# The tail of a one-core hybrid layer: last down products by column halves, gate rows and final gain spread by TensorE

## The reference, cut to what matters

```python
xf = x + gate1 * mix                                   # x1
h = rmsnorm(xf, norm2_g) * (1 + scale2) + shift2
act = silu(g) * u * combine.T[:, :, None]
routed = einsum('etf,efd->td', act, w_expert_down)
xf = xf + gate2 * (routed + shared)
y = rmsnorm(xf, final_norm_g)
```

## Time and profile before

| what | value |
|---|---|
| median of three runs | 862.09 us (861.97 to 862.58) |
| the profiled execution | 862.36 us, span 860.5 us |
| granted TensorE clock, mean | 0.982 |
| PE busy | 809.0 us (94%) |
| DVE busy | 385.1 us (45%) |
| ACT busy | 238.9 us (28%) |
| DMA read and written | 280.67 MB, 3.16 MB |

### The profile page before, as it was taken

How to read it: one execution, slowest core, us unless ns; L and a number is a source line. 1 busy time by engine, 2 the same in 40 slices (tenths; PEclk the granted TensorE clock), 3 DMA queues, 4 the chain that set the end, 5 groups by cost and what they waited for, 6 DMA issues and landing times.

```text
span 860.5 us, 13102 instructions
## 1 busy us (share of the span) xinstructions
PE 809.0 (94%) x5330; PEld 556.9 (65%) x5330; DVE 385.1 (45%) x789; ACT 238.9 (28%) x397; POOL 20.0 (2%) x22
## 2 busy tenths in 40 slices
PE   3999999999999989999999999699999999799974
PEld 1788989999999979964545445254554835355212
DVE  1157899879987657573232312122221111112014
ACT  2253747535345144231111111011121101011002
POOL 1000010100000010100000000000000000000000
PEclk9999999999999999999999999899999999899998
DMA  8998877432443739978999999999999999999995
GB/s 322 387 387 299 299 271 283 162 125 98 145 150 101 230 119 375 369 294 341 364 415 418 416 417 418 414 418 419 415 417 410 418 413 419 417 417 418 417 414 205
DMA packets 81223, 284.71 MB, mean 331 GB/s; under 512 B 5257, under 2 KB 12041, under 8 KB 64521
## 3 DMA queue, kind: packets, MB, share of 16 engines
q1 hardware_dynamic: 80664, 282.55, 84.5%
q10 hardware_dynamic: 496, 1.30, 0.4%
HBM read 280.67 MB, written 3.16 MB: 330 GB/s over the span
## 4 chain that ended last, share of the span: by engine, by line
PE 72%; SPq 14%; DMA 9%; DVE 3%; issue 2%; ACT 0%; POOL 0%; DVEq 0%; POOLq 0%
PE bank L2118 13%; SPq L620 13%; PE bank L2174 7%; PE bank L1708 6%; PE bank L1713 6%; PE bank L1710 6%; DMA chunk<-in_w_expert_down 5%; PE bank L2002 4%; PE bank L2025 3%; PE bank L1694 3%; PE bank L1770 3%; DMA chunk<-in_w_expert_gate_up 3%; PE bank L1655 3%; PE bank L1752 3%; PE bank L1730 2%; PE bank L1734 2%
## 5 line engine op out<-in xcount | busy, mean ns | idle before, releaser
L2118 PE MATMUL bank<-chunk,xg 128*64 128x512 f32 (+2 forms) x1024 | 202.5, 624 | 19.8 <-DMA chunk<-in_w_expert_gate_up 19.6
L2118 PEld LDWEIGHTS bank<-chunk,xg 128*64 128x64 f32 (+2 forms) x1024 | 62.7, 131 | 153.1 <-issue 137.1
L2174 PE MATMUL bank<-chunk,act_t 128*64 128x512 f32 (+2 forms) x480 | 95.7, 597 | 1.5 <-DMA chunk<-in_w_expert_down 1.5
L1509 DVE SCALAR_TENSOR_TENSOR act_r<-bank,w_slot,sil 128x256 f32<-128x256 f32 x26 | 12.6, 484 | 182.6 <-ACT sil L984 182.6
L984 ACT ACTIVATE sil<-bank 128x256 f32<-128x256 f32 x26 | 10.0, 384 | 211.3 <-PE bank L2118 211.3
L1521 DVE TENSOR_TENSOR y_lo<-bank,y_hi 128x512 fp32r<-128x512 f32 x52 | 35.9, 691 | 72.2 <-ACT y_hi L997 72.2
L1077 DVE TENSOR_TENSOR ring_lo<-ring,ring_hi 128x1024 fp32r<-128x1024 f32 x44 | 52.6, 1219 | 18.3 <-ACT ring_hi L766 18.1
L2174 PEld LDWEIGHTS bank<-chunk,act_t 128*64 128x64 f32 (+2 forms) x480 | 29.6, 127 | 46.9 <-issue 46.0
L997 ACT ACTIVATE y_hi<-bank 128x512 fp32r<-128x512 f32 x52 | 30.9, 597 | 100.5 <-PE bank L2174 95.7
L1137 DVE SCALAR_TENSOR_TENSOR conv<-upad,dw,conv 128x256 f32<-128x256 f32 x120 | 52.8, 511 | 0.0
L766 ACT ACTIVATE ring_hi<-ring 128x1024 fp32r<-128x1024 f32 x44 | 44.4, 1051 | 24.8 <-PE bank L1734 14.9
(11 more groups left out here) (319 smaller groups left out, 1239.2 us busy)
## 6 DMA issues: line engine op xcount, KB each, us to landing
chunk<-in_w_expert_gate_up SPq DMA_DIRECT2D x128, 1024.0 KB, 20.9
chunk<-in_w_expert_down SPq DMA_DIRECT2D x63, 1024.0 KB, 22.7
ring<-in_w_in SPq DMA_DIRECT2D x16, 2048.0 KB, 9.9
ring<-in_w_ada SPq DMA_DIRECT2D x12, 2048.0 KB, 14.8
ring<-in_w_proj_hgrn SPq DMA_DIRECT2D x2, 2048.0 KB, 7.9
ring<-in_w_out SPq DMA_DIRECT2D x2, 2048.0 KB, 13.0
ring<-in_w_proj_conv SPq DMA_DIRECT2D x1, 2048.0 KB, 7.7
chunk<-in_w_shared_gate_up SPq DMA_DIRECT2D x2, 1024.0 KB, 23.0
```

The lines of the kernel that those rows point to most:

```text
L2118: ins = mm(bank[2 + b][row:row + width, :], xg[:, k, c:c + width], w[:, k % 4, :], start=(k == 0), stop=(k == KD - 1))
L2174: ins = mm(out[row:row + width, :], act_t[:, c, row:row + width], w[:, c, h * 512:(h + 1) * 512], start=(c == 0), stop=(c == 1))
```

## The change

1. The last chunk is loaded in two column halves, each holding both contraction halves (128 x 2 pieces of 2 KB). `last_down` makes output half 0 first and reports it, then half 1, with the wait for the second piece in front of the last expert's product of half 1.
2. `finish` on PE scatters half 0, waits for `x1_back`, makes two of the four groups of `x1` transposes, then waits for half 1, scatters it and makes the other two groups. `gated_y` waits for its own half alone.
3. `gate2` and the final gain are no longer loaded in spread form. PE makes the six rows of 512 columns in `final_rows`, between the two gate and up halves of the last step: 24 float32 products of a broadcast column with the identity, in banks 0 and 1 by turns. ACT copies each out.
4. `final_norm_g` becomes a twelfth small load (8 rows), in the place of the convolution's weights. These become the last load on ACT's queue.
5. The DRAM copy of the modulation holds `shift2` alone: one transpose fewer, and half the copy and the store.
6. The `x1` load waits for place 16 alone and is the only load behind the last chunk.

```diff
-R_ALL = 116
+R_FG = 116
+R_ALL = 124
 ...
-                       (by_row(A["conv_norm_b"][0]), rows[R_CNB:R_CNB + 4, :]),
+                       (by_row(A["conv_norm_b"][0]), rows[R_CNB:R_CNB + 4, :]), (by_row(A["final_norm_g"]), rows[R_FG:R_FG + 8, :]),
                        (A["conv_dw_w"][0].rearrange("w (c p) -> (w c) p", p=P), rows_dw[0:CW * CC, :])]
 ...
-                        for c, loaded_half in enumerate((s_chunk[place_of(number)], s_last_half)):
-                            src = dn_src[bass.ds(experts[item], 1)][:, :, c:c + 1, :].rearrange("a p c d -> (a p) c d")
-                            sp.dma_start(dn_tile(place_of(number))[:, c:c + 1, :], src).then_inc(loaded_half, 16)
-            for number in (max(n for n in CHUNK_AT if place_of(n) == at_) for at_ in FINAL_PLACES):
-                freed(number)
-            for s in range(NS):
-                sp.dma_start(g2row[:, s, :].rearrange("p (k c) -> p k c", k=KD), mod_row(1, s)).then_inc(s_g2_back, 16)
+                        for hf, loaded_half in enumerate((s_chunk[place_of(number)], s_last_half)):
+                            c = slice(hf * 512, (hf + 1) * 512)
+                            src = dn_src[bass.ds(experts[item], 1)][:, :, :, c].rearrange("a p c d -> (a p) c d")
+                            sp.dma_start(dn_tile(place_of(number))[:, :, c], src).then_inc(loaded_half, 16)
+            freed(max(n for n in CHUNK_AT if place_of(n) == FINAL_X1))
             sp.dma_start(x1_back[:, :, :].rearrange("p k t -> p (k t)"), A["x1"]).then_inc(s_x1_back, 16)
-            sp.dma_start(fin_g[:, :], A["final_norm_g"].rearrange("(a d) -> a d", a=1).broadcast_to([P, D])).then_inc(s_x, 16)
 ...
                 if n == NSTEPS - 1:
+                    for j in range(6):
+                        c = slice(j % 2 * 512, (j % 2 + 1) * 512)
+                        act.wait_ge(row_made, j + 1)
+                        nc.scalar.activation(g2row[:, j // 2, c] if j < 4 else fin_g[:, c], bank[j % 2][:, :], ACT.Copy).then_inc(row_kept, 1)
 ...
-                    dve.wait_ge(y_done, 3 + s)
+                    dve.wait_ge(y_done, 2 * hf + s + 1)
 ...
-                dve.wait_ge(s_x, 48)
 ...
-                dve.wait_ge(s_g2_back, 32)
+                dve.wait_ge(row_kept, 6)
 ...
+            def final_rows():
+                pe.wait_ge(pt_evac, NSTEPS)
+                for j in range(6):
+                    if j >= 2:
+                        pe.wait_ge(row_kept, j - 1)
+                    s, hf = divmod(j, 2)
+                    for i in range(4):
+                        k = 4 * hf + i
+                        col = mod_v[:, M_GT2 + k, s:s + 1] if j < 4 else vec[:, R_FG + k:R_FG + k + 1]
+                        ins = mm(bank[hf][:, i * P:(i + 1) * P], col.broadcast_to([P, P]), ident, start=True, stop=True)
+                    ins.then_inc(row_made, 1)
 ...
+                    if (n, half) == (NSTEPS - 1, 0):
+                        final_rows()
 ...
-                for h in range(2):
-                    for c in range(2):
-                        for item in range(items - c):
-                            one(h, c, item)
-                pe.wait_ge(s_last_half, 16)
-                for h in range(2):
-                    one(h, 1, items - 1).then_inc(dn_done, 1)
+                for c in range(2):
+                    for item in range(items):
+                        ins = one(0, c, item)
+                ins.then_inc(dn_done, 1)
+                for c in range(2):
+                    for item in range(items):
+                        if (c, item) == (0, items - 1):
+                            pe.wait_ge(s_last_half, 16)
+                        ins = one(1, c, item)
+                ins.then_inc(dn_done, 1)
 ...
-                for h in range(2):
-                    pe.wait_ge(y_ready, 2 * NSTEPS - 1 + h)
-                    for s in range(NS):
-                        scatter(1, s, h, last=True).then_inc(y_done, 1)
+                pe.wait_ge(y_ready, 2 * NSTEPS - 1)
+                for s in range(NS):
+                    scatter(1, s, 0, last=True).then_inc(y_done, 1)
                 pe.wait_ge(s_x1_back, 16)
-                for j in range(4):
+                for j in range(2):
+                    x1_to_tokens(j)
+                pe.wait_ge(y_ready, 2 * NSTEPS)
+                for s in range(NS):
+                    scatter(1, s, 1, last=True).then_inc(y_done, 1)
+                for j in range(2, 4):
                     x1_to_tokens(j)
```

More of the change, by code:

```diff
@@ L82 @@
 FINAL_PLACES = (15, 16, 17)
+FINAL_X1 = 16
 LOADS_BEFORE_EXTRAS = (len(CHUNK_NO) - EXTRA_PLACES) // NCHUNK + 1
@@ L85 @@
 assert len(CHUNK_NO) % NCHUNK >= EXTRA_PLACES
+assert all(max((n, key) for n, key in CHUNK_AT.items() if n % NCHUNK == place)[1][0] == NSTEPS - 2 for place in FINAL_PLACES)
 C_ID, C_MASK = 0, P
@@ L191, in build @@
         c_pad = at("c_pad", 205, [P, KD, 32])
-        mod_cols = at("mod_cols", 205, [NS * KD, 2 * P])
+        mod_cols = at("mod_cols", 205, [NS * KD, P])
         b_router = at("b_router", 207, [P, NE])
@@ L264, in build @@
         mod_v = mod[:, :, :]
-        s_x, s_cst, s_rows, s_s0, s_wr = map(sem, ("x_and_final_gain_loaded", "consts_loaded", "rows_loaded", "s0_then_shift_rows_loaded", "masks_router_and_routing_consts_loaded"))
+        s_x, s_cst, s_rows, s_s0, s_wr = map(sem, ("x_loaded", "consts_loaded", "rows_loaded", "s0_then_shift_rows_loaded", "masks_router_and_routing_consts_loaded"))
         gain1_done, u1_bias_ready, u1_part_ready = map(sem, ("gain1_done", "u1_bias_ready", "u1_bias_rows_made_then_copied"))
@@ L307, in build @@
         s_last_half = sem("last_half_chunk_loaded")
-        g2_ready, g2_evac = sem("gate2_ready"), sem("gate2_evac")
-        s_g2_kept, s_g2_back = sem("gate2_stored"), sem("gate2_loaded")
+        sh2_ready, sh2_evac, s_sh2_kept = sem("shift2_ready"), sem("shift2_evac"), sem("shift2_stored")
+        row_made, row_kept = sem("final_row_made"), sem("final_row_kept")
         cnt_ready, nx_done, end_ready, oh_done = map(sem, ("count_ready", "nx_done", "end_ready", "onehot_done"))
@@ L564, in _ @@
             sp.dma_start(new_state[0, 0].rearrange("a h k v -> k (a h) v"), s_new[:, :, :]).then_inc(s_state, 16)
-            sp.wait_ge(g2_evac, 1)
-            sp.dma_start(A["mod_rows"], mod_cols[:, :]).then_inc(s_g2_kept, 16)
+            sp.wait_ge(sh2_evac, 1)
+            sp.dma_start(A["shift_rows"], mod_cols[:, :]).then_inc(s_sh2_kept, 16)
             def load_fixed(number):
@@ L571, in load_fixed @@
                 load_part(number, part, FIRST_FIXED + sum(ITEMS_OF[:step]) + item)
-            def mod_row(m, s):
-                return A["mod_rows"].rearrange("(k s) (m c) -> s m k c", s=NS, m=2)[s:s + 1, m].broadcast_to([P, KD, P])
             for number in range(NCHUNK):
@@ L579, in _ @@
                     sp.wait_ge(o_ready, 4)
-                    sp.wait_ge(s_g2_kept, 16)
+                    sp.wait_ge(s_sh2_kept, 16)
                     for s in range(NS):
-                        sp.dma_start(shift_row[:, s, :].rearrange("p (k c) -> p k c", k=KD), mod_row(0, s)).then_inc(s_s0, 16)
+                        src = A["shift_rows"].rearrange("(k s) c -> s k c", s=NS)[s:s + 1].broadcast_to([P, KD, P])
+                        sp.dma_start(shift_row[:, s, :].rearrange("p (k c) -> p k c", k=KD), src).then_inc(s_s0, 16)
                 if number == 5:
@@ L884, in _ @@
                             nc.scalar.activation(upad_row[:, c * T:(c + 1) * T], conv[:, c, :], ACT.Sigmoid).then_inc(cs_done, 1)
-            act.wait_ge(g2_ready, 1)
-            nc.scalar.activation(mod_cols[:, :], bank[7][0:NS * KD, 0:2 * P], ACT.Copy).then_inc(g2_evac, 1)
+            act.wait_ge(sh2_ready, 1)
+            nc.scalar.activation(mod_cols[:, :], bank[7][0:NS * KD, 0:P], ACT.Copy).then_inc(sh2_evac, 1)
             act.wait_ge(cb_ready, 1)
@@ L1340, in _ @@
             dve.wait_ge(s_state, 16)
-            dve.wait_ge(s_g2_kept, 16)
+            dve.wait_ge(s_sh2_kept, 16)
             own.mark(V.memset(selm, -BIG))
@@ L1633, in _ @@
             pe.wait_ge(s_cst, 32)
-            pe.wait_ge(s_rows, 16 * 11)
+            pe.wait_ge(s_rows, 16 * 12)
             nc.tensor.transpose(bank[7][:, 0:R_ALL], rows[0:R_ALL, :], ident[0:R_ALL, 0:R_ALL])
@@ L1834, in _ @@
                     pe.wait_ge(mod_done, 7)
-                    nc.tensor.transpose(bank[7][0:NS * KD, 0:P], mod_v[:, M_SH2:M_SH2 + KD, :].rearrange("p k s -> p (k s)"), ident)
-                    nc.tensor.transpose(bank[7][0:NS * KD, P:2 * P], mod_v[:, M_GT2:M_GT2 + KD, :].rearrange("p k s -> p (k s)"), ident).then_inc(g2_ready, 1)
+                    nc.tensor.transpose(bank[7][0:NS * KD, 0:P], mod_v[:, M_SH2:M_SH2 + KD, :].rearrange("p k s -> p (k s)"), ident).then_inc(sh2_ready, 1)
                 if level == 4:
@@ L2326 @@
     aps["consts_x"] = nc.dram_tensor("in_consts_x", (P, X_ALL), F32, kind="ExternalInput").ap()
```

(2 more changed lines are left out.)

## The result

The changed kernel takes 865.55 us, the median of seven runs (864.06 to 867.64). The kernel before took 862.11 in seven runs (861.51 to 864.5; the three of the table of before are among them). The ratio is 1.0038, 95% interval 1.0028 to 1.0049: 3.4 us slower, where 1.2 us faster was forecast. The profiled execution took 865.55 us and has a span of 863.7 us, 3.2 more than before.

The account below looks back on a forecast made before the run. The stream of weights was taken to set the time, with a tail behind the last chunk's landing. Tail -1.35, start +0.3 and one transpose -0.1 gave -1.15 us: 860.9 us, with 8 in 10 from 859.7 to 862.6.

Parts of the forecast that it names:

- tail: From the last down products to `residual(0)`: split halves overlap the work, `residual(0)` at 849.31 instead of 850.66, gain 1.35 us.
- start: Before the first modulation product: convolution's rows, now last on ACT's queue, land later; 0.3 us taken between 0 and 1.4.
- one transpose: One transpose fewer where PE is dense, 0.1 us gained; the halved copy and store move nothing.
- bound of 1.4: Late end for the start: load shares engines with the modulation weights to 10.96, so the start is at 12.5.
- The sentence from the Trainium skill about 4 engines: Convolution's load at the start: 124 rows split over 4 DMA engines, making the sum some 0.5 us worse.
- Rival C: At the start: the delay is paid in full, 1.1 us more than in the sum, 862.0, no change; chance 0.10.
- rival B: Before the last down products: PE's clock falls, products cost 1.6 to 2.5 us more, 862.5 to 863.4; chance 0.10.
- nearer the short ones: PE's 2.2 us wait before the last down products, judged closer to 1.46 and 1.55 us waits, followed by fast products.
- Half 0's copy: In the tail: ACT's first copy of the down products' results comes some 2.0 us after PE's start.
- D: In the tail: `x1` lands late, 848.5, half 1's scatter waits, the gain is gone, 862.3; chance 0.08.
- Rival A: Last chunk's first piece lands earlier without `g2row` packets, 0.6 to 1.3 us more gain, say 860.0; chance 0.22.
- All three signs: Clock 0.50 behind 842 us; last piece over 0.7 us from 842.3; first modulation product behind 12 us.

Follow-up runs that it names:

- experiment 3: Two variants of the changed kernel, each run once for start times: convolution's rows first on ACT's queue, or last but cut in two; rows complete at 9.34 and 9.80 us.
- rows_split: Changed kernel with the convolution's rows back last on SP's queue and the final gain's two rows made behind the last activation's transposes: 860.54 us, ratio 0.9982.
- wide_fill_behind: `start_mended` plus two unused wide float32 products behind the last activation's transposes, the six rows kept together in the first wait: 860.86 us, ratio 0.9983.
- wide_fill_before: `tail_alone` plus five unused wide float32 products in the wait for the second half's weights; run once, last down products 5.10 us, no total given.
- tail_alone: Kernel before with column halves, the new `finish` order and gating by bank; `gate2` rows and gain still loaded, behind `x1`: 862.26 us, ratio 0.9998.
- the first of experiment 3: Changed kernel with the convolution's rows as first small load on ACT's queue, run once: rows complete at 9.34 us, modulation product at 11.61.
- start_mended: Changed kernel with the convolution's rows again last on SP's queue and the final gain's rows last on ACT's: 861.88 us, ratio 1.0001.
- the second of experiment 3: Changed kernel with the convolution's rows still last on ACT's queue but cut into loads of 112 and 12 rows, run once: rows complete at 9.80 us.
- one_group_ahead: `rows_split` with one group of `x1` transposes, not two, in front of half 1's scatter; run on another chip: 861.14 us, ratio 0.9994.

## Why the prediction was wrong

The sum was -1.35 (tail) + 0.3 (start) - 0.1 (one transpose) = -1.15 us; the result is +3.4.

**The start: the term that failed.** It was put at 0.3, with a bound of 1.4, and it is 3.0 (11.10 to 14.09); alone it costs 3.2 us of the total by the medians. The bound let the load share its engines "to their end (10.96)" and took that end for fixed. In the changed kernel the modulation weights, issued at 3.04, themselves landed 8.9 us later, at 11.9, and the load landed behind them, at 12.35. That is 1.4 us beyond the bound's end. From the landing to the product it was 1.7 us, where the forecast's 12.5 had 1.5. The load's own 8.75 us are 4.3 us before its first packet at 7.9, 3.7 us of turns, four rows at a time (experiment 3), and the rest to the landing. The weights land between 10.9 and 11.5 in the kernels without such a load beside them, and at 11.9 in the two with it; that the load itself holds them back is argued, not shown.

The sentence from the Trainium skill about 4 engines pointed to the late end. The forecast took 0.3 against it, a value that it read from no row. The packets of experiment 3, four at a time, bear the page out. Rival C had the right place and too small a price, as it used the same bound.

**The clock: rival B came true.** The wait before the last down products was forecast at 2.2 us and is 2.44. The rows (no fall behind 1.55, a fall behind 4.41) left it open, and "nearer the short ones" decided wrongly. The products cost 1.67 us more (5.34 for 3.67), inside B's 1.6 to 2.5. That eats the tail's gain. With 3.0 for 0.3 at the start and 1.7 for the clock, the forecast's 860.9 becomes 865.3; 865.55 was measured. B and C were given 0.10 each and were taken for alternatives; both happened at once, and more than C.

**What held.** The tail's arithmetic: 6.73 us forecast from the products' start to the `x1` addition, 6.86 measured in `rows_split`, where the clock stays; so the gain is 1.3 us for 1.35. Half 0's copy at 2.0 us was 1.98. `final_rows` took 5.7 us (831.04 to 836.71) for 5.8. `final_rows` fills the first wait, and the second half then takes 3.64 us. `x1` (issued at 832.71, landed 15.8 later, at 848.5) was there before PE asked at 851.36. PE asked late there, but in `rows_split`, at full clock, `x1` also landed 1.0 us ahead (issued at 829.19, 15.7 later, at 844.9; asked for at 845.95), which puts D aside. Rival A falls too: with no `g2row` packets T0, the landing of the last chunk's first piece, came 2.55 us later than before, where PE's stream at 827 was 2.4 late.

All three signs that the prediction set for being wrong appeared: clock 0.50 behind 842 us, the piece at 844.82 and not near 842.3, and the modulation product at 14.09.

**How it adds up.** In the profiles: the start gives +3.3 at 30 us, of which 3.0 are the later product. One transpose fewer takes 0.1. At 380 us the clock did not fall this time (below), which takes 0.8. T0 is then 2.55 late, 0.15 more than these give; what adds that isn't known. The tail adds 0.4, and `residual(0)` starts 2.95 later. The span is 3.2 longer; the last 0.25 lie behind `residual(0)` and are not traced to a cause.

## What to carry to other kernels

A small load at the start of this kernel was priced by three things that its size does not show: what was queued ahead of it and beside it, how its outer dimension divided over the DMA engines, and what stood between its landing and the first large product. A bound that uses the end of another transfer must ask whether that end moves too. Before work is moved into one of TensorE's waits, look at the next wait: the one that grows can cost the clock, and the same work cut in two can keep both short. A loss that cancels a gain looks like a change without effect. Neither the tail alone nor the change with its start mended was faster than the kernel before; only the runs with the second wait filled as well showed that a tail worth 1.3 us was in it.

## What the runs showed of the hardware that was not expected

**The clock.** Last down products behind idleness of 0.98, 1.34, 1.38, 1.71 us took 3.64 (and 3.67 behind 1.55); behind 2.44, 2.59, 2.71 and 2.74 they took 5.34, behind 3.26 they took 5.10 (2.59 and 2.71 are the two kernels of experiment 3). The down products of an earlier step, at 561 us, show the same at shorter waits: 3.64 us behind 1.36 to 1.56 in eight kernels, 5.34 behind 1.76 (`wide_fill_behind`), 1.94 (`rows_split`) and 2.08 (`wide_fill_before`). Timeline of `tail_alone`, then of `rows_split`:

```profile
562.30 3.64 PE L2175 MATMUL bank<-chunk,act_t 128*32 128x512 f32 x32 [1.47 <-DMA chunk<-in_w_expert_down]
```

```profile
560.76 5.34 PE L2194 MATMUL bank<-chunk,act_t 128*32 128x512 f32 x32 [1.94 <-DMA chunk<-in_w_expert_down]
```

So the 2.2 us of the forecast was no safe wait, and in these two steps 1.7 is the longest that was. But the length of the wait is not all that counts. The second group of 16 modulation products, at 20 to 23 us, took 1.92 us behind 2.40 to 2.46 us of idleness in four kernels (`rows_split`, `wide_fill_before`, `wide_fill_behind` and the first of experiment 3), and 3.51 to 3.62 behind only 1.64 to 1.76 in three (the changed kernel, `start_mended` and the second of experiment 3). In the other four it was 2.56 to 2.73 behind 2.60 to 2.61. What the granted clock depends on besides is open.

**The same code at another clock.** The first gather (380 to 384 us) ran at 0.66 before, at 1.00 in the changed kernel, `start_mended` and `rows_split`, and at 0.64 in `one_group_ahead`. In the changed kernel this made good 0.8 us of the start's 3.3: the delay was 3.26 us at 375 and 2.41 at 387. `tail_alone` and `wide_fill_before` are alike up to 827 us and ran on the same chip, at 0.66 and 1.00 there, so neither this code nor the chip explains the fall. From 22 to 26 us they ran at 0.71 and 1.00. At 824 us (first half of the last gate and up products, 824.3 against 822.8) the first was 1.5 us behind the second. Differences of up to 1.5 us between single profiles of this kernel can be this alone.

**Small loads beside a large one.** The last small load of ACT's queue let PE begin at these times. Four rows, issued at 3.25 us: 7.29 to 7.58. Eight rows, issued at 3.60: 8.56, 8.72, 8.90 and 9.40, in four kernels with the same start. Eight rows, issued at 3.85: 9.34. Twelve rows, issued at 3.97 behind the 112: 9.80. An issue 0.35 us later, with four rows more, thus put PE's start off by 1.0 to 2.1 us, and the same load at the same issue varied by 0.8.
